# Third merge with its first two rounds' gate blocks ahead of their y blocks, and VectorE's steps of the mLSTM heads in another order

## The reference

```python
def token_mixer(xn, w_in, ...):
    lru_in, fox_qkv, fox_f, ml_qkv, ml_if, ml_o, gate_in = split_columns(xn @ w_in)
    ...
    yc = mlstm_mixer(mqkv[:, :, 0], mqkv[:, :, 1], mqkv[:, :, 2], ..., ml_o, m_nw)
    g = jax.nn.sigmoid(gate_in + gate_b).reshape(B, S, N_BRANCHES, D_MODEL)
    merged = g[:, :, 0] * (ya @ w_br_lru) + g[:, :, 1] * (yb @ w_br_fox) + g[:, :, 2] * (yc @ w_br_mlstm)
    return merged @ w_out

# in mlstm_mixer, per head
h = num / jnp.maximum(jnp.abs(den), jnp.exp(-m_t))[..., None]
h = head_layer_norm(h, norm_w)          # h - mean, times rsqrt(variance + eps)
return h * jax.nn.sigmoid(o_pre)

# per layer
x = x + token_mixer(rms_norm(x, norm1_w[l]), ...)
x = x + peer_ffn(rms_norm(x, norm2_w[l]), ...)
```

## Time and profile before

| | us |
|---|---|
| median of 3 runs | 4485.99 (4482.55 to 4495.91) |
| the profiled execution | 4483.62 |
| its span in the profile | 4481.7 |
| PE busy | 4291.1 (96%) |
| VectorE busy | 3080.0 (69%) |
| POOL busy | 2706.3 (60%) |
| ACT busy | 1809.7 (40%) |

### The profile page before, as it was taken

One profiled execution on the slowest core, in us unless ns is written; L12 is line 12 of the kernel. 1 busy time (PEld: TensorE's weight loads), 2 busy tenths in 40 slices (PEclk: granted clock), 3 DMA queues, 4 the chain that ended last, 5 costly groups with the idle time before them and its releaser, 6 DMA issues.

```text
span 4481.7 us, 74541 instructions
## 1 busy us (share of the span) xinstructions
PE 4291.1 (96%) x21290; PEld 3668.2 (82%) x21290; DVE 3080.0 (69%) x5391; ACT 1809.7 (40%) x3324; POOL 2706.3 (60%) x1505
## 2 busy tenths in 40 slices
PE   8999999999999999999999999989999999999998
PEld 6777876779999997787777778767899999977777
DVE  6666435547788767888866654365487887588888
ACT  4145023124576653333331540231246776533333
POOL 6843764665577665555568438637655776645554
PEclk9999999999999999999999999999999999999999
DMA  3233944734599998999722339347246999989997
GB/s 107 90 108 100 276 141 132 204 106 136 194 350 348 319 308 306 337 344 336 285 83 91 110 99 296 123 127 235 83 142 214 349 359 311 302 297 341 337 333 270
DMA packets 494906, 1011.79 MB, mean 226 GB/s; under 512 B 51536, under 2 KB 320464, under 8 KB 491856
## 3 DMA queue, kind: packets, MB, share of 16 engines
q1 hardware_dynamic: 420656, 739.77, 51.1%
q0 software_dynamic: 73728, 268.47, 16.6%
q10 hardware_dynamic: 288, 1.05, 0.1%
HBM read 846.57 MB, written 162.53 MB: 225 GB/s over the span
## 4 chain that ended last, share of the span: by engine, by line
PE 77%; DMA 7%; DVE 6%; issue 4%; ACT 3%; POOL 1%; SPq 1%; DVEq 0%; ACTq 0%; POOLq 0%
PE bank L1351 13%; PE pair L1008 7%; PE bank L1355 6%; PE bank L1008 6%; PE bank L1408 6%; PE bank L1413 5%; DMA ring<-v_tab 5%; PE bank L1403 5%; PE pair L1010 3%; PE bank L1382 3%; PE bank L1010 3%; PE pair L1034 3%; PE bank L1034 2%; PE bank L1075 2%; PE pair L1075 2%
## 5 line engine op out<-in xcount | busy, mean ns | idle before, releaser
L861 POOL TENSOR_TENSOR w_hi<-ring,ones 128x1024 fp32r<-128x1024 f32 x272 | 542.0, 1993 | 723.5 <-PE bank L1034 235.9
L1351 PE MATMUL bank<-xT,w_hi 128*128 128x384 f32 x2048 | 710.1, 347 | 5.6 <-ACT w_hi L1815 3.4
L864 POOL TENSOR_TENSOR w_lo<-ring,w_hi 128x1024 fp32r<-128x1024 f32 x272 | 692.9, 2548 | 21.4
L1351 PE MATMUL bank<-xl_peer,w_hi 128*128 128x384 f32 x2048 | 689.4, 337 | 0.0
L849 POOL TENSOR_TENSOR w_lo<-ring,w_hi 128x1024 fp32r<-128x1024 f32 x192 | 463.3, 2414 | 305.0 <-ACT w_hi L1815 304.3
L1821 ACT CAST w_hi<-ring 128x1024 fp32r<-128x1024 f32 x252 | 265.5, 1054 | 660.1 <-PE bank L1413 440.1
L2672 DVE TENSOR_TENSOR cl<-att,ch 128x384 fp32r<-128x384 f32 x256 | 350.7, 1370 | 167.7 <-ACT ch L1890 154.3
L855 POOL TENSOR_TENSOR w_lo<-ring,w_hi 128x1024 fp32r<-128x1024 f32 x126 | 301.9, 2396 | 268.6 <-ACT w_hi L1821 268.6
L1408 PE MATMUL bank<-w_hi,cl 128*128 128x512 f32 x1524 | 391.9, 393 | 17.0 <-DVE cl L2672 16.9
L1403 PE MATMUL bank<-w_hi,ch 128*128 128x512 f32 x1524 | 389.0, 391 | 17.6 <-ACT ch L1890 17.4
L1355 PE MATMUL bank<-xT,w_lo 128*128 128x384 f32 x2048 | 396.9, 334 | 0.0
(11 more groups left out here) (400 smaller groups left out, 9378.2 us busy)
## 6 DMA issues: line engine op xcount, KB each, us to landing
ring<-v_tab SPq DMA_DIRECT2D x252, 512.0 KB, 6.3
ring<-w_stream SPq DMA_DIRECT2D x240, 512.0 KB, 3.8
g_spill<-gst SPq DMA_DIRECT2D x240, 192.0 KB, 4.5
vg<-w_spill SPq DMA_DIRECT2D x64, 704.0 KB, 10.5
att<-u_tab SPq DMA_DIRECT2D x320, 128.0 KB, 4.5
u_turned<-att SPq DMA_DIRECT2D x80, 512.0 KB, 5.6
ring<-u_tab SPq DMA_DIRECT2D x256, 128.0 KB, 3.2
ring<-u_turned SPq DMA_DIRECT2D x64, 512.0 KB, 5.6
```

The costliest lines, as they stand in the source:

```text
L861: nc.gpsimd.tensor_tensor(w_hi[b][:, 0:n], src, ones[:, 0:1].to_broadcast([P, n]), ALU.mult)\
L864: nc.gpsimd.tensor_tensor(w_lo[b][:, 0:n], src, w_hi[b][:, 0:n].bitcast(F32), ALU.subtract)\
L1351: nc.tensor.matmul(out, w_hi[s % 2][:, c * P:(c + 1) * P], dense_parts(c)[part], start=(c == 0 and part == 0), stop=False)
```

## The change

**The order in which weights arrive.** Through the ring, phase MC's round 0 is now the gate blocks of rounds 0 and 1, and its round 1 the y blocks of rounds 0 and 1 (`gates_then_values`). Rounds 2 and 3 are as before. Every block is still loaded, split and multiplied once.

```diff
+            def gates_then_values(L, n, beside):
+
+                at = 4 * ROUND0["MC"] + 2 * n
+                load_round(L, ROUND0["MC"] + n, lambda s: w_stream[L * NSTREAM + (at + 4 * (s // 2) + s % 2)], beside=beside)
...
+                stream_round(L, r0, begin)
+                if ph == "MQ":
+                    stream_round(L, r0 + 1, going_on(1))
+                    gates_then_values(L, 0, going_on(2))
+                    gates_then_values(L, 1, end)
+                else:
+                    with sp.Fori(1, count // 4) as j:
+                        stream_round(L, j + r0, going_on(j))
+                    stream_round(L, r0 + count // 4, end)
```

```diff
+                    for s in range(2, 4):
+                        project(L, "MC", 0, s, x_parts(xl_mix))
                     pe.wait_ge(y_lo_ready.sem, y_lo_ready.at(L, "MQ", 2, 1))
-                    for s in range(2, 4):
-                        pe.wait_ge(split_ready.sem, split_ready.at(L, "MC", 0, s + 1))
-                        pe.wait_ge(drained_sem[s], drnd(L, "MC", 0) + 1)
+                    for s in range(2):
+                        pe.wait_ge(split_ready.sem, split_ready.at(L, "MC", 1, s + 1))
+                        pe.wait_ge(drained_sem[s], drnd(L, "MC", 1) + 1)
                         terms(s, range(KC - 2))
                     pe.wait_ge(y_lo_ready.sem, y_lo_ready.at(L, "MQ", 3, 1))
-                    for s in range(2, 4):
+                    for s in range(2):
                         terms(s, (KC - 2,))
                     pe.wait_ge(y7_lo_ready.sem, y7_lo_ready.at(L, "MQ", 0, 1))
+                    for s in range(2):
+                        terms(s, (KC - 1,)).then_inc(proj_done, 1)
                     for s in range(2, 4):
-                        terms(s, (KC - 1,)).then_inc(proj_done, 1)
+                        project(L, "MC", 1, s, y_parts(y_hi))
 
                 last_heads()
                 stand(pe)
-                with pe.Fori(1, 4) as i:
+                with pe.Fori(2, 4) as i:
                     for s in range(4):
                         project(L, "MC", i, s, x_parts(xl_mix) if s < 2 else y_parts(y_hi))
```

```diff
                         floors(i + 1, 1)
+                def early_gate(s):
+
+                    proj_wait(L, "MC", 0, s)
+                    nc.scalar.activation(qk[:, s, :], bank[s][:, :], ACT.Tanh, scale=0.5,
+                                         bias=dcol(hb, 4 * KC + s)).then_inc(drained_sem[s], 1)
+
+                early_gate(0)
+                early_gate(1)
                 act.wait_ge(ml_y.sem, ml_y.at(L, "MQ", 3, 1))
                 nc.scalar.copy(y_hi[:, 6, :], yT[:, 6, :]).then_inc(y_hi_ready.sem, 1)
                 act.wait_ge(ml_y.sem, ml_y.at(L, "MQ", 3, 2))
                 nc.scalar.copy(y_hi[:, 7, :], yT[:, 7, :]).then_inc(y7_hi_ready.sem, 1)
-                merge_gates(L, "MC", 2)
+                early_gate(2)
+                early_gate(3)
+                for i in range(2):
+                    merged_high(L, i)
+                merge_gates(L, "MC", 2, 2)
```

```diff
-                def divide(c, i):
-
-                    for p in range(2):
...
+                def divide(c, i, p):
+
+                    dve.wait_ge(dev_ready.sem, dev_ready.at(L, "MQ", i, p + 1))
...
                 def heads(c, i):
-                    denominator(c, i, 0)
+
+                    c.n = 1
                     denominator(c, i, 1)
                     decay_mask(i + 1, 0)
                     turn_single(L, "MQ", i, 0)
+                    variance(i, 0)
                     decay_mask(i + 1, 1)
-                    variance(i, 0)
                     variance(i, 1)
                     turn_single(L, "MQ", i, 1)
                     weigh(i + 1, 0)
                     weigh(i + 1, 1)
+                    divide(c, i, 0)
                     turn_single(L, "MQ", i, 2)
-                    divide(c, i)
+                    denominator(c, i + 1, 0)
+                    divide(c, i, 1)
                     turn_single(L, "MQ", i, 3)
+                    c.n -= 1
                     c.close()
 
                 def last_heads(c):
-                    denominator(c, 3, 0)
+
+                    c.n = 1
+                    denominator(c, 3, 1)
                     low_part(L, "MQ", 0, y_lo, yT, y_hi, 1)
-                    denominator(c, 3, 1)
-                    for n in range(1, 3):
-                        low_part(L, "MQ", n, y_lo, yT, y_hi, 1)
                     variance(3, 0)
+                    low_part(L, "MQ", 1, y_lo, yT, y_hi, 1)
                     variance(3, 1)
-                    divide(c, 3)
+                    low_part(L, "MQ", 2, y_lo, yT, y_hi, 1)
+                    divide(c, 3, 0)
+                    divide(c, 3, 1)
...
+                denominator(Chain(dve, dve_step, L, "MQ", 0), 0, 0)
                 with dve.Fori(0, 3) as i:
                     heads(Chain(dve, dve_step, L, "MQ", i), i)
                 last_heads(Chain(dve, dve_step, L, "MQ", 3))
+                def merge_tile(t):
+
+                    dve.wait_ge(proj_done, slots_done(L, "MC", 1, t + 1))
+                    dve.wait_ge(drained_sem[t], drnd(L, "MC", 0) + 2)
+                    dve.wait_ge(merged_ready.sem, merged_ready.at(L, "MC", t // 2, t % 2))
+                    V.scalar_tensor_tensor(out=mtmp, in0=qk[:, t, :], scalar=1.0, in1=bank[t][:, :],
+                                           op0=ALU.add, op1=ALU.mult).then_inc(drained_sem[t], 1)
+                    dve.wait_ge(drained_sem[t], drnd(L, "MC", 1) + 2)
+                    V.tensor_tensor(merged[:, t, :], merged[:, t, :], mtmp, ALU.add).then_inc(merged_ready.sem, 1)
+
+                merge_tile(0)
+                merge_tile(1)
+                low_part(L, "MC", 0, m_lo, merged, m_hi, 1)
                 turn_ahead(L, AHEAD_AT["MC"], 0)
-                merge_round(L, "MC", 1, lambda: turn_ahead(L, AHEAD_AT["MC"] + 1, 1))
+                merge_tile(2)
+                turn_ahead(L, AHEAD_AT["MC"] + 1, 1)
+                merge_tile(3)
+                low_part(L, "MC", 1, m_lo, merged, m_hi, 1)
```

More of the change, by code:

```diff
@@ L599, in begin, with going_on @@
                     ahead_load(L, first + s, s, single_raw[ph])
-                stream_round(L, r0, begin)
-                with sp.Fori(1, count // 4) as j:
+                def going_on(j):
                     def go_on(s):
@@ L605, in go_on @@
                         ahead_load(L, 4 * j + (first + s), s, single_raw[ph])
-                    stream_round(L, j + r0, go_on)
+                    return go_on
                 def end(s):
@@ L611, in end @@
                         ahead_store(L, first + count - 1, 1, single_turned)
-                stream_round(L, r0 + count // 4, end)
+                stream_round(L, r0, begin)
[7 more added lines that the diff above has]
+                    stream_round(L, r0 + count // 4, end)
             def ahead_rounds(L, r0, first, count):
@@ L1522, in gate, with merged_high @@
                     .then_inc(drained_sem[j], 1)
+            def merged_high(L, i):
+                act.wait_ge(merged_ready.sem, merged_ready.at(L, "MC", i, 2))
+                nc.scalar.copy(m_hi[:, ds(2 * i, 2), :], merged[:, ds(2 * i, 2), :]).then_inc(y_hi_ready.sem, 1)
             def merge_gates(L, ph, branch, begun=0):
@@ L1528, in merge_gates @@
                     if ph == "MC":
-                        act.wait_ge(merged_ready.sem, merged_ready.at(L, "MC", i, 2))
-                        nc.scalar.copy(m_hi[:, ds(2 * i, 2), :], merged[:, ds(2 * i, 2), :]).then_inc(y_hi_ready.sem, 1)
+                        merged_high(L, i)
             with act.Fori(0, DEPTH) as L:
@@ L2311, in _ @@
                 decay_mask(0, 1)
-                def divide(c, i):
-                    for p in range(2):
-                        dve.wait_ge(dev_ready.sem, dev_ready.at(L, "MQ", i, p + 1))
-                        c.step(V.reciprocal(em[:, p, :], em[:, p, :]))
-                        c.wait()
-                        c.step(V.tensor_tensor(hh[:, p, :], hh[:, p, :], em[:, p, :], ALU.mult))
-                        c.wait()
-                        V.tensor_tensor(yT[:, 2 * i + p, :], hh[:, p, :], og[:, 2 * i + p, :], ALU.mult)\
-                            .then_inc(ml_y.sem, 1)
+                def divide(c, i, p):
+                    dve.wait_ge(dev_ready.sem, dev_ready.at(L, "MQ", i, p + 1))
+                    c.step(V.reciprocal(em[:, p, :], em[:, p, :]))
+                    c.wait()
+                    c.step(V.tensor_tensor(hh[:, p, :], hh[:, p, :], em[:, p, :], ALU.mult))
+                    c.wait()
+                    V.tensor_tensor(yT[:, 2 * i + p, :], hh[:, p, :], og[:, 2 * i + p, :], ALU.mult)\
+                        .then_inc(ml_y.sem, 1)
                 def heads(c, i):
-                    denominator(c, i, 0)
+                    c.n = 1
                     denominator(c, i, 1)
@@ L2360, in _ @@
                 last_heads(Chain(dve, dve_step, L, "MQ", 3))
```

(8 more changed lines are left out.)

## The result

| | before | changed |
|---|---|---|
| median, runs behind the prediction's comparison | 4482.69 (6) | 4449.66 (6) |
| the same comparison again, later (below) | 4484.98 (17) | 4455.54 (6) |
| profiled execution's span | 4481.7 | 4441.0 |

The change makes the kernel 0.73% faster: ratio 0.9927, 95% interval 0.9913 to 0.9940; the second comparison gives 0.9930 (0.9913 to 0.9947). That is 29 to 33 us by the medians, where 23 were forecast, and the intervals of both comparisons (some 27 to 39 and 24 to 39 us) lie above 23. The direction was right, and so were the waits that went and came; the clock's part was too small.

What follows compares the result with a forecast made beforehand. PE, at 77%, was taken to bound the kernel. Net waits 16.6, clock 5.0 and OUT 1.6 sum to 23.2, taking 4483.6 to 4460.4; the median stands 2.4 above, so 4463, range 4455 to 4477.

Steps and rivals of the forecast that it cites:

- the clock's part: Shorter PE waits leave less low clock, in the pairs (1.6) and behind `y_lo` (3.4): 5.0 us, ends 0 and 8.
- Waits that go: PE's waits at q1 (7.0), the second denominator (5.2) and `y_lo` of head 6 (2.7) vanish: 14.9 us per layer.
- What is late next: New PE waits per layer: second head's spread M for ACT's floor 5.2, last pair's q0 and second y block 1.4.
- OUT: End of the third merge: OUT's second round waits less for VectorE's take-out, 0.8 us per layer, 1.6 in all.
- VectorE's queue: Pair loop: the second division ends 2.8 us later behind the early denominator; G keeps 3.0 of room, cost nothing.
- Rival C: Slower: second division, ACT's copy and G slip beyond the 3.0 of room, PE stands at G; 4499, chance 0.05.
- the slow sixteen matmuls behind: Third merge, after POOL's wait of 4.1: 6.50 us instead of 3.63, expected again at the same price, no gain.
- A: The wait comes back on ACT, each spread M waiting 2.1 to 2.8; near 4476, chance 0.18.
- The chance of 4479: ACT's table loads each cost about 1.38 us more for a drain, some 16.6 in six pairs; chance 0.02.
- B: The end is held elsewhere or the order takes no effect, OUT's waits growing; 4478 to 4486, chance 0.09.
- unseen waits: Waits without a profile row, last pair's q0 (0.6) and second y block (0.8); range end 0 to 4.1 each way.

Runs made afterwards that it cites:

- ACT's floors are first: Changed kernel with ACT's two floors and last key block of the next pair ahead of the pair's two roots; ratio to before 0.9901.
- the means' part: Changed kernel with denominators and divisions back at their places of before, only variance(i, 0) ahead of the second mask; profile only, both stretches 619.3 us.
- both further edits: Changed kernel with ACT's floors ahead of the roots and the third merge's first y block finished early; 4434.85 against 4483.95 before, ratio 0.9896.

## Where the prediction held, and where it failed

- **Waits that go (14.9 per layer)**: all three, in both layers.
- **What is late next (5.2 + 1.4)**: 5.5, 0.4, 0.5. The chain on ACT was the right one, to 0.1 per wait (1.6, 1.6, 2.3 against 1.5, 1.5, 2.2). Net waits with OUT: 18.1 by the sums, forecast 16.6 + 1.6 = 18.2. That the totals agree so well has some luck in it, as OUT fell 1.0 short.
- **VectorE's queue**: the second division ends at 734.67 in the third pair, ACT's copy at 735.35, and PE takes G at 737.98 without a wait: 2.6 of room, forecast 3.0. Rival C needed it gone.

```profile
728.31 0.69 DVE L2329 TENSOR_TENSOR att<-bank,floor 128x512 f32<-128x512 f32 x1 [2.80 <-PE bank L1249]
...
733.98 0.69 DVE L2349 TENSOR_TENSOR big<-att,vg 128x512 f32 x1 [0.26 <-DVE att L2347]
```

- **OUT**: 3.0 and 2.2 became 2.5 and 2.1, that is 0.6 in place of 1.6. Within its ends, but 2.5 lies outside the 1.4 to 2.2 that the profile was to show, and the second profiles (3.9 and 2.1 before, 2.1 and 2.8 changed) say that this wait moves by up to 0.9 between executions.
- **The clock: the step that failed.** It was put at 5.0, with an end at 8; it measured 10.3 (11.9 by low places at 1.7 each). The two parts in the 5.0 came as forecast: three low places in the pairs became two (1.7), and both behind `y_lo` went (3.4). The rest had been put at nothing. First, the text moved "the slow sixteen matmuls behind" POOL's wait along "at the same price". They took 6.50 and 6.18 before (layers 0 and 1) and 5.53 in both layers now, 1.6 less together: a double low place became a single one in each layer, and the second profiles of both kernels repeat that. Secondly, OUT's second round had a low place in each layer, which the clock's part did not mention; both are gone, another 3.4.

Why these two parts went stays open. That the clock before answered to both waits, the 2.7 for `y_lo` and POOL's 4.1, would be an explanation for the first, but other rows speak against it. With no wait for `y_lo` at all the sixteen matmuls take 6.07 and 6.22 once ACT's floors are first, and 6.35 in one layer of the means' part. Changed kernel, then ACT's floors first, layer 0:

```profile
812.10 5.53 PE pair L1019 x16
```

```profile
807.49 6.07 PE pair L1019 x16
```

At OUT the waits changed by 0.5 and 0.1, and waits of that length have a low place behind them in some executions and not in others. So the forecast's error was to give the low clock one fixed price at one wait and none at the other; how much of the 5 us between 5.0 and 10.3 is the new order's and how much is luck, these runs don't say.

- **The rivals**: A's mark, 4476, needed M waits of 2.1 to 2.8 and low clock as before; the waits are 1.6 in four of six pairs, with full clock behind them. The chance of 4479 rested on a drain beside each table load, as the Trainium skill gives it (page "ScalarE: Activation LUTs", section "What ACT_TABLE_LOAD costs"). It fell too: the measured chain has no room for the drain. B: OUT did not grow. C: no wait at G.
- **The range**: the ends that the text names (clock 0 to 8, OUT 0 to 5.2, unseen waits 0 to 4.1 each) add up to gains of 3 to 33, while it gives 15 to 31. With 10.3 for the clock the forecast's sum gives 4458, inside the range, so the clock alone doesn't put 4449.7 outside it. Before's own median was 3.3 lower in the comparison (4482.7), and the other 5 us are spread between executions, for which the range had no term: the second comparison's median is 4455.5. That this number and not the other fell outside is luck.

## What to carry to other kernels

When a change removes waits of 2 us and more from TensorE, price the clock behind each of them from the profile's clock column, all the way to the next long wait, and give it ends of its own: the same matmuls behind a wait of some 4.2 took 5.4 to 6.5 us here, and the same wait of 2.2 had a low place behind it in one layer and not in the other. A wait that appears in place of another should be traced to the chain that ends it: here a reorder of three calls on ACT, which the forecast's own chain had pointed at, was worth as much as half of the change. A weight buffer of this kernel is given back by its last matmul, so with two buffers finish one block rather than bring both to the end side by side.

## What the runs showed of the hardware

**When the clock falls.** In the 13 profiles of this study, in the two stretches and the wait that ends each, PE stood between 1.2 and 1.6 us 45 times, and none of these waits had the lower level behind it (once it came 5.3 later, inside the next wait). After waits of 2.0 to 2.4 it came 27 times in 52, after 2.5 to 3.0 46 times in 60, after the 20 of 3.9 to 4.3 always, and for twice as long in nine of them. The same wait of the same kernel can have it in one layer and not in the other (POOL's 2.2 in the kernel with both further edits: with it in layer 0, without it in layer 1). What decides between them is left open here. Outside the stretches the two profiles of the changed kernel differ by 14.7 us with the same code: 11.1 of it is low clock and 3.3 are PE's waits. So this lottery is also much of the spread between executions. The counts fit with what was seen when three waits of 2.1 to 2.8 were traded for two of 1.6 and one of 2.3: 4.6 us in the stretches, of which the waits are 3.

**Filling a wait cost no time that could be seen, and bought none**: with 26 extra matmuls per layer the kernel before has a ratio of 0.9992 (0.9979 to 1.0006), although the clock at the filled place rose from 0.74 to 1.00.
